# Sums of squares of q from a weight of ones in four column strips, and two transposes, in a hybrid decoder block

## The reference, cut to what matters

```python
def l2norm(t):
    return t * lax.rsqrt(jnp.sum(t * t, axis=-1, keepdims=True) + NORM_EPS)
...
    qkv = jax.nn.silu(causal_depthwise_conv(qkv_raw.astype(f32), conv_w.astype(f32)))
    q, k, v = jnp.split(qkv, [GDN_HEADS * GDN_DK, 2 * GDN_HEADS * GDN_DK], axis=-1)
    qc = l2norm(to_chunks(q, GDN_HEADS, GDN_DK, c)) * (GDN_DK ** -0.5)
    kc = l2norm(to_chunks(k, GDN_HEADS, GDN_DK, c))
```

```python
    mod = (c_act @ ada_w[l] + ada_b[l])[:, None, :]
```

## Time and profile before

| | us |
|---|---|
| median of 3 runs | 2617.77 |
| lowest, highest | 2617.58, 2618.81 |
| the profiled execution | 2619.01 |
| its span in the trace | 2617.3 |
| PE busy in the span | 2548.7 (97%) |
| DVE busy | 1897.2 (72%) |
| ACT busy | 992.2 (38%) |

### The profile page before, as it was taken

The page is one execution under the profiler, slowest core; times in us unless marked ns, Lnnn a source line. Parts: engine busy times, 40 slices in busy tenths (PEclk is TensorE's granted clock), DMA queues, the critical chain, the costliest instruction groups (busy, mean ns, idle before and its releaser), DMA issues.

```text
span 2617.3 us, 44201 instructions
## 1 busy us (share of the span) xinstructions
PE 2548.7 (97%) x16256; PEld 2263.4 (86%) x16256; DVE 1897.2 (72%) x3610; ACT 992.2 (38%) x2216; POOL 504.1 (19%) x440
## 2 busy tenths in 40 slices
PE   5999999999999999999999999999999999999998
PEld 3899899889889989989989998989888888888887
DVE  5588778878878887777777777785666666666666
ACT  5544654564474474355345345333400000000002
POOL 1000411310220140000000000000254443333330
PEclk9999999999999999999999999999999999999999
DMA  7211231122122113123213213332121111111111
GB/s 224 71 56 37 51 86 41 33 76 67 26 76 64 25 50 86 42 53 82 45 35 95 50 34 89 78 109 75 49 59 47 48 49 49 49 49 49 49 41 65
DMA packets 221703, 160.85 MB, mean 61 GB/s; under 512 B 24720, under 2 KB 204024, under 8 KB 221488
## 3 DMA queue, kind: packets, MB, share of 16 engines
q1 hardware_dynamic: 208592, 149.98, 19.7%
q0 software_dynamic: 12896, 8.05, 3.1%
HBM read 141.67 MB, written 16.33 MB: 60 GB/s over the span
## 4 chain that ended last, share of the span: by engine, by line
PE 78%; DVE 13%; ACT 6%; issue 1%; DMA 1%; SPq 0%; DVEq 0%; ACTq 0%
PE bank L180 32%; PE bank L172 20%; PE bank L2180 9%; PE bank L1245 2%; PE bank L998 2%; PE bank L1251 2%; DVE sig L1078 2%; PE bank L1579 1%; PE bank L1594 1%; PE bank L1597 1%; PE bank L1595 1%; PE bank L1202 1%; DVE rows_region L1087 1%; PE bank L1745 1%; DVE sig L1076 1%
## 5 line engine op out<-in xcount | busy, mean ns | idle before, releaser
L172 PE MATMUL bank<-wA_hi,h_hi 128*128 128x256 f32 x1024 | 296.7, 290 | 0.9 <-ACT sig L1050 0.4
L172 PE MATMUL bank<-wB_hi,h_hi 128*128 128x256 f32 x1024 | 296.6, 290 | 0.5 <-ACT feat_region L1035 0.3
L172 PE MATMUL bank<-wB_lo,h_hi 128*128 128x256 f32 x1024 | 295.7, 289 | 0.0
L172 PE MATMUL bank<-wA_lo,h_hi 128*128 128x256 f32 x1024 | 295.5, 289 | 0.0
L172 PE MATMUL bank<-wB_hi,h_lo 128*128 128x256 f32 x1024 | 295.3, 288 | 0.0
L172 PE MATMUL bank<-wA_hi,h_lo 128*128 128x256 f32 x1024 | 295.3, 288 | 0.0
L180 PE MATMUL bank<-h_hi,wA_hi 128*128 128x512 f32 x672 | 267.3, 398 | 7.1 <-ACT glr_t L1025 4.8
L180 PE MATMUL bank<-h_hi,wA_lo 128*128 128x512 f32 x672 | 266.8, 397 | 0.0
L180 PE MATMUL bank<-h_lo,wA_hi 128*128 128x512 f32 x672 | 266.5, 397 | 0.0
L180 PE MATMUL bank<-h_hi,wB_lo 128*128 128x512 f32 x672 | 265.9, 396 | 0.0
L180 PE MATMUL bank<-h_hi,wB_hi 128*128 128x512 f32 x672 | 265.8, 396 | 0.0
(11 more groups left out here) (393 smaller groups left out, 6047.6 us busy)
## 6 DMA issues: line engine op xcount, KB each, us to landing
w_raw<-in_w_in_dram SPq DMA_DIRECT2D x96, 512.0 KB, 4.0
w_raw<-in_w_ffn_up_dram SPq DMA_DIRECT2D x44, 512.0 KB, 3.9
rows_region<-in_ada_w_dram SPq DMA_DIRECT2D x64, 256.0 KB, 2.8
...
```

What stands on the lines that cost most here:

```text
L172: mm = nc.tensor.matmul(bank[:, n_out:n_out + n1 - n0], (h_hi, h_lo)[hp][:, k, t * P:t * P + P], buf[wp][:, k, n0:n1], start=(s == 0), sto ...
```

## The change

The sums of k stay as they are (though in columns 0 to 7 of the bank, and read apart). The sums of q are made in another way:

- at offset 14 PE makes 4 products in place of 8: the weight is a block of ones of 32 columns, the moving operand a quarter of the squares (256 tokens), each on another column strip of the array. All 32 partitions of a strip then hold the same row of 256 sums;
- at offset 16 (`Q_LN`) ACT takes the logarithm of the 128x256 block, out of the bank into the place of the squares in `conv_in`;
- at offset 18 (`Q_TURN`) PE turns the two halves with two transposes of 128x128 into the same bank;
- at offset 20 (`Q_COL`) ACT copies 8 columns out of them into `lnss` (one of every 32 columns);
- the logarithm of k's sums covers 8 columns, and PE's sums of k also wait for ACT's copy of q (`gate_ln`), since they write where it read;
- `conv_ss` of q, for which the convolution of v waits on ACT, is now signalled by the transposes, four beats later than the sums.

The two semaphores that this needs are taken from the loads of `ada_w`: two loads share one, and each `ada_pe` waits for both loads of its pair.

```diff
@@ ada_load, ada_pe
-        sp.dma_start(ada_buf[m][:], ada_v[:, :, o:o + ADA_W]).then_inc(sem(f"ada_in{m}"), 16)
+        sp.dma_start(ada_buf[m][:], ada_v[:, :, o:o + ADA_W]).then_inc(sem(f"ada_in{m // 2}"), 16)
...
-        pe.wait_ge(sem(f"ada_in{m}"), 16)
+        pe.wait_ge(sem(f"ada_in{m // 2}"), 32)
...
+    SUM_N = S // (P // STRIP)
+    Q_LN, Q_TURN, Q_COL = SS + 2, SS + 4, SS + 6
@@ conv_act
+            elif o == Q_LN and j == 0:
+                act.wait_ge(sem("q_sum"), i + 2)
+                step(A(e[:, 0:SUM_N], M[5][:, 0:SUM_N], ACT.Ln, bias=eps[:]), "q_row")
+            elif o == Q_COL and j == 0:
+                act.wait_ge(sem("conv_ss"), 2 * (i + 1) + 1)
+                by_strip = M[5][:, 0:SUM_N].rearrange("p (c s x) -> p s c x", c=SUM_N // P, x=STRIP)[:, :, :, 0]
+                step(A(lnss[:, 0].rearrange("p (s c) -> p s c", c=SUM_N // P), by_strip, ACT.Copy), "gate_ln")
@@ conv_pe
-        for j in range(2):
-            if r == CONV_AT[i][j] + SS:
-                pe.wait_ge(sem("conv_sq"), 2 * (i + 1) + j + 1)
-                if j == 0 and i >= 0:
-                    pe.wait_ge(sem("gdn_y"), NT * (i + 1))
-                for t in range(NT):
-                    sq = conv_in[:, j, GDN_TAPS - 1:]
-                    mm = nc.tensor.matmul(M[5][:, j * NT + t:j * NT + t + 1], sq[:, t * P:t * P + P], ones[:, 0:1],
-                                          start=True, stop=True)
-                mm.then_inc(sem("conv_ss"), 1)
+        o = r - CONV_AT[i][0]
+        sq = conv_in[:, 0, GDN_TAPS - 1:]
+        if o == SS:
+            pe.wait_ge(sem("conv_sq"), 2 * (i + 1) + 1)
+            if i >= 0:
+                pe.wait_ge(sem("gdn_y"), NT * (i + 1))
+            for n in range(P // STRIP):
+                mm = nc.tensor.matmul(M[5][n * STRIP:n * STRIP + STRIP, 0:SUM_N], ones[:, 0:STRIP],
+                                      sq[:, n * SUM_N:n * SUM_N + SUM_N], start=True, stop=True,
+                                      tile_position=(0, n * STRIP))
+            mm.then_inc(sem("q_sum"), 1)
+        elif o == Q_TURN:
+            pe.wait_ge(sem("q_row"), i + 2)
+            for n in range(SUM_N // P):
+                tp = nc.tensor.transpose(M[5][:, n * P:n * P + P], sq[:, n * P:n * P + P], ident[:])
+            tp.then_inc(sem("conv_ss"), 1)
+        if r == CONV_AT[i][1] + SS:
+            pe.wait_ge(sem("conv_sq"), 2 * (i + 1) + 2)
+            pe.wait_ge(sem("gate_ln"), 2 * (i + 1) + 1)
+            sq = conv_in[:, 1, GDN_TAPS - 1:]
+            for t in range(NT):
+                mm = nc.tensor.matmul(M[5][:, t:t + 1], sq[:, t * P:t * P + P], ones[:, 0:1], start=True, stop=True)
+            mm.then_inc(sem("conv_ss"), 1)
@@ gates_act
-            step(nc.scalar.activation(lnss[:].rearrange("p q t -> p (q t)"), M[5][:, 0:2 * NT], ACT.Ln,
-                                      bias=eps[:]), "gate_ln")
+            step(nc.scalar.activation(lnss[:, 1], M[5][:, 0:NT], ACT.Ln, bias=eps[:]), "gate_ln")
```

2 lines of the change are left out of this document (1 added, 1 removed).

## The result

The changed kernel took 2625.25 us (median of 11 runs, 2622.27 to 2628.80) against 2617.59 for the kernel before, timed beside it (11 runs, 2616.50 to 2619.08): a ratio of 1.0027, 95% interval 1.0019 to 1.0035. A second comparison gave 2624.80 (2622.72 to 2627.99) against 2618.55, 1.0024 (1.0015 to 1.0033).

What follows compares the result with a forecast made beforehand. PE holds 78% of the chain, but q's sums have almost no room on it. Prologue 1.9, lead-in 0, four GLA rounds x 0.26, three mLSTM rounds x 0.65: 4.9 later, 2622.7 us (+0.19%), range 2618.5 to 2626.0.

Steps and rivals of the forecast that it cites:

- the 1.24 a head: q's sums on PE: four strip products at 0.47 in place of 1.71 save 1.24 us per head.
- the 0.20: mLSTM rounds, start of zg1: PE can keep at most 0.20 us of its saving before waiting for ACT's L1035.
- some seven slow transposes: Prologue, second half of x's transposes: about seven run at the lower clock after the pause, 0.7 us.
- The bound of 0.4: Prologue, paired loads: lower bound of the 1.9 us delay, if the clock is up for the first product too.
- The 1.2: Prologue: the second ada_w load lands at 26.5, so the second half of x's transposes starts 1.2 us late.
- the rival in which it comes before 24.8: Costs taken up: load before 24.8 or prologue delay vanishing, mLSTM rounds losing only 0.26; 1.8 us later, 2619.6; chance 0.18.
- The rival with all 32 transposes at the lower clock: Prologue: clock stays low through x's 32 transposes, prologue 4.5 us, in all 7.5 later, 2625.3; chance 0.14.
- The wait of about 1.3 ahead of zg1: GLA rounds, profile sign: PE idles about 1.3 us ahead of zg1, ended by ACT's L1035.
- there PE is already waiting for ACT: mLSTM round, k's sums: they start 0.06 us behind the end of k's squares on ACT, so PE already waits.
- The ACT idle of 0.93 ahead of L1609: mLSTM rounds: ACT's 0.93 us idle, waiting for PE, takes up the 0.4 us of Q_LN's logarithm.
- The chance of 0.57: Whole kernel: probability that the time stays within 0.2% (5.2 us) of the kernel before, counted as the same.
- more is lost: Rival: restarts cost 0.1 each, logarithm takes 0.6, more prologue work at the lower clock; 2626.5 us; chance 0.07.

Runs made afterwards that it cites:

- the second trace: The changed kernel, unchanged, timed and profiled once more: median 2624.80 us against 2618.55 for the kernel before, its profiled execution 2626.61.
- e9: Changed kernel with own semaphores for the first two ada_w loads, plus ten dummy transposes ahead of q's strip products in every head: 2622.15 us against 2618.81, 1.0013.
- e3: Kernel before with q's eight narrow products replaced by one product of eight columns, seven sums left out: 2622.12 us against 2618.26, 1.0012.
- e10: e3 with ten dummy transposes ahead of q's one product: 2618.71 us against 2618.81 for the kernel before, 1.0000.
- e1: Changed kernel with own semaphores for the first two ada_w loads, the other loads still in pairs: 2622.20 us against 2618.26 for the kernel before, 1.0016.
- the busy wait: Changed kernel with twelve dummy transposes on PE ahead of its wait for the first pair of ada_w loads: 2621.51 us against 2618.26, 1.0012.
- e5: e1 without the two transposes of q's sums, the copy taking a row of the strips instead: 2621.46 us against 2618.81 for the kernel before, 1.0013.
- e15: e1 with Q_COL one beat earlier, at SS + 5 in place of SS + 6: 2622.68 us against 2618.55 for the kernel before, 1.0015.

## Why the prediction was right, and where it was wrong

**The saving on PE: mechanism right, its price missed.** That none of the 1.24 a head would arrive is borne out. The strips take 0.57 to the next instruction where 0.47 was taken, so 1.1 is saved; in round 0 PE is 1.0 ahead of the kernel before at 315 us and 0 ahead at 320, and in round 4 it keeps 0.1 of the 0.20. But the prediction priced the unused saving at nothing: "What becomes of it: in GLA rounds 0". It can cost: PE waits in place of working, and behind the wait the clock sometimes falls. Shown is this for the larger saving: one product in place of eight cost 3.9 us in the median, and ten dummies gave it back. For the change itself it is small: one of the three falls of the second trace stands at this place, 1.0 us, it is the only one in eight traces, and filling the wait (e9) brought at most 0.6, within the noise.

**Behind k's sums: missed.** Two of the three falls, 1.5 and 1.0 us, stand behind k's sixteen narrow steps in an mLSTM round, which now come behind a pause of 0.2. The traces show pause, narrow steps and fall in this order five times in four traces, and no fall behind k's sums where the pause is absent; that the pause makes the fall is argued from this count, e3 and e10 and not shown here, since the kernel that filled it did not get faster.

**The paired loads: mechanism right, the clock's term too small.** 1.9 was taken, as 1.2 for the late load and 0.7 for the clock. Between the two traces in which DVE was ready at the same time (the changed kernel and e1) it is 1.4 and 1.9 on the transposes, 3.3 at their end, 2.6 at head 0; over all traces 3.3. So the late start was about right, and the term that was mis-sized is the "some seven slow transposes": 1.93 is the price of about 18. In the second trace, where DVE was ready at 25.18 and the load landed at 27.2, the same two are 4.0 and 1.05. The bound of 0.4 with the clock up for the product too is what the busy wait shows, at 0.14. The 1.2 was right in size only: the load landed at 25.3, not at 26.5, and DVE was ready 1.3 earlier as well. In all fourteen traces it landed between 25.1 and 27.5, so the rival in which it comes before 24.8 has no case. The rival with all 32 transposes at the lower clock did not come true either; by the rows the clock returned within them, and that its 2625.3 meets the median is a coincidence.

**Two transposes in a GLA round: right.** 0.26 forecast, about 0.2 found for head 1 and 0.19, 0.23 and 0.21 for heads 2 to 4, and 0 in e5 without them. The wait of about 1.3 ahead of zg1 that was to be seen is split and has another releaser in its larger part: in the changed kernel's first trace PE sat idle ahead of L172 as follows (us in total, times, longest us), so 0.56 a time for DVE's L1131 and 0.25 a time for ACT's L1035.

```profile
PE bank L172 <- DVE wB_lo L1131: 2.2, 4, 0.6
...
PE bank L172 <- DVE wA_lo L1131: 1.7, 3, 0.6
...
PE bank L172 <- ACT feat_region L1035: 1.0, 4, 0.3
```

**An mLSTM round: total right, two terms wrong and one path missed.** 0.65 forecast, 0.66, 0.76 and 0.47 found. Q_LN took 0.48 and not 0.38, Q_COL 0.21 with its gap and not 0.30; the errors cancel. In round 4, ACT is 0.50 late at L1042 by Q_LN, 0.44 at L1609, and 0.65 at the squares with the copy. PE's waits are not where they were to be seen: 0.48 inside zg0 for DVE's L1131 and 0.1 ahead of zg1, where 1.0 was forecast; the 0.3 ahead of the transposes is there. The reading "there PE is already waiting for ACT" was not so: in the rows of before PE came to k's sums just as the squares ended. That cost the sum nothing, since the turn makes PE 0.45 late (0.35 forecast, the difference is the longer Q_LN) and the copy on ACT adds the other 0.2. The step "The ACT idle of 0.93 ahead of L1609 ... takes the 0.4 up again" holds for L1609 itself but not for the round, as e5 showed: DVE waited for the sigmoid step right behind Q_LN all the time, and through it and L1623 0.3 reaches k's squares without any turn on PE. That the copy sits ahead of k's squares was not the point either: a beat earlier costs the same (e15). In round 4 ACT has no idle time between L1623 and the squares that the copy could take.

**The lead-in: just over its bound.** 0 (0 to 0.2) forecast, 0.27 found in the solve of head 0, in every trace with the new sums; what it is made of was not followed.

**The sum.** 4.9 by the profiled execution, 4.8 found in the first. That this is so close is partly luck: the prologue's term was too small, and the trace of before, with its late x and its slow stretches behind 1750 us, was a long one to compare with. To the medians the sum is short by 1.4 to 2.8, and the falls of the clock in the rounds are of that size (3.5 in one trace, 0 in another); that they make the difference is an estimate, for late row DMAs spread the runs as well (last section). The chance of 0.57 for "within 0.2%" went to the wrong side; "more is lost" named the lower clock, but in the prologue.
